# A wait in the adaLN weight ring and the order of VectorE's work around the first softmax are changed in a two-block transformer kernel

## The reference, cut to what matters

```
# first block, mixer
proj = rmsnorm(x) @ w_in                      # gq gk gr gv | mq mk | gg (gate) | mv
o_gla  = rmsnorm(gla_chunked(...)) * silu(gg) # 4 heads of 128, gated linear attention
o_moba = softmax attention over mq, mk, mv    # 8 heads of 64, causal
x = x + (concat([o_gla, o_moba]) * mix_scale) @ w_out
x = x + peer_ffn(...)
# second block, conditioning (adaLN)
mod   = silu(c) @ ada_w[l] + ada_b[l]         # ada_w[l]: 1024 x 6144, two layers
mod_c = silu(c_ctx) @ ada_w[l] + ada_b[l]
```

## Time and profile before

| what | value |
|---|---|
| median of three runs | 1842.73 us (1839.59, 1842.73, 1842.90) |
| the profiled execution | 1842.73 us, span 1840.8 us |
| TensorE matmul busy | 94% of the span |
| VectorE, ScalarE busy | 66%, 52% |
| transfers | 316 MB, mean 172 GB/s |
| mean granted TensorE clock | 0.979 of full |

### The profile page before, as it was taken

How to read it: one execution, slowest core, us unless ns; L and a number is a source line. 1 busy time by engine, 2 the same in 40 slices (tenths; PEclk the granted TensorE clock), 3 DMA queues, 4 the chain that set the end, 5 groups by cost and what they waited for, 6 DMA issues and landing times.

```text
span 1840.8 us, 37954 instructions
## 1 busy us (share of the span) xinstructions
PE 1739.4 (94%) x13770; PEld 1632.6 (89%) x13770; DVE 1211.6 (66%) x2411; ACT 949.5 (52%) x1824; POOL 77.2 (4%) x74
## 2 busy tenths in 40 slices
PE   7898999999999888999999999988999999889997
PEld 6765999999999755899999999976899999889997
DVE  5446558888854599755555566457676666767666
ACT  5444555555554588555555554337554445445442
POOL 0000000000000166100000000000000000000000
PEclk9989999999999899999999999999999999999999
DMA  6535445556556578555565555410355564546553
GB/s 235 199 138 194 149 149 177 178 182 182 177 178 185 202 283 289 172 183 182 186 203 182 182 182 155 152 44 1 115 181 182 183 207 144 155 138 183 182 182 103
DMA packets 86936, 316.38 MB, mean 172 GB/s; under 512 B 9664, under 2 KB 9808, under 8 KB 86352
## 3 DMA queue, kind: packets, MB, share of 16 engines
q1 hardware_dynamic: 85248, 309.30, 52.4%
q10 hardware_dynamic: 1328, 4.01, 0.6%
q0 software_dynamic: 288, 2.10, 0.3%
HBM read 314.32 MB, written 1.05 MB: 171 GB/s over the span
## 4 chain that ended last, share of the span: by engine, by line
PE 88%; DVE 6%; ACT 2%; issue 2%; DMA 2%; ACTq 0%; POOLq 0%; DVEq 0%
PE bank L494 30%; PE acc L494 21%; PE bank L495 15%; PE acc L495 11%; PE bank L852 4%; PE acc L571 3%; PE bank L592 1%; ACT arena L1099 1%; DMA route<-in_ada_w 1%; DVE w_lo L1584 1%; DVE small L2073 1%; ACT w_hi L1099 1%; PE bank L811 0%; ACT L1099 0%; DVE arena L2094 0%
## 5 line engine op out<-in xcount | busy, mean ns | idle before, releaser
L1584 DVE TENSOR_TENSOR w_lo<-raw,w_hi 128x512 fp32r<-128x512 f32 x982 | 652.2, 688 | 462.2 <-ACT w_hi L1099 459.5
L1099 ACT ACTIVATE w_hi<-raw 128x512 fp32r<-128x512 f32 x982 | 591.8, 626 | 429.7 <-PE acc L494 267.1
L494 PE MATMUL bank<-x_hi,w_hi 128*128 128x256 f32 x2224 | 637.1, 286 | 24.0 <-DVE w_lo L1584 17.1
L494 PE MATMUL bank<-x_lo,w_hi 128*128 128x256 f32 x2224 | 633.3, 285 | 0.0
L495 PE MATMUL bank<-x_hi,w_lo 128*128 128x256 f32 x2224 | 633.1, 285 | 0.0
L494 PEld LDWEIGHTS bank<-x_hi,w_hi 128*128 128x128 f32 x2224 | 430.1, 193 | 30.9 <-issue 17.1
L494 PEld LDWEIGHTS bank<-x_lo,w_hi 128*128 128x128 f32 x2224 | 430.4, 194 | 0.2 <-issue 0.2
L495 PEld LDWEIGHTS bank<-x_hi,w_lo 128*128 128x128 f32 x2224 | 430.4, 194 | 0.0
L494 PE MATMUL acc<-x_hi,w_hi 128*128 128x256 f32 x1024 | 290.6, 284 | 1.4 <-issue 1.4
L494 PE MATMUL acc<-x_lo,w_hi 128*128 128x256 f32 x1024 | 290.5, 284 | 0.0
L495 PE MATMUL acc<-x_hi,w_lo 128*128 128x256 f32 x1024 | 290.4, 284 | 0.0
(11 more groups left out here) (258 smaller groups left out, 1566.1 us busy)
## 6 DMA issues: line engine op xcount, KB each, us to landing
raw<-in_peer_u SPq DMA_DIRECT2D x128, 512.0 KB, 3.5
raw<-in_peer_v SPq DMA_DIRECT2D x128, 512.0 KB, 3.5
raw<-in_mlp_w SPq DMA_DIRECT2D x128, 512.0 KB, 3.6
ada_x<-in_ada_w SPq DMA_DIRECT2D x64, 512.0 KB, 4.2
route<-in_ada_w SPq DMA_DIRECT2D x32, 512.0 KB, 5.3
raw<-in_w_in SPq DMA_DIRECT2D x25, 512.0 KB, 4.5
raw<-in_conv_w_in SPq DMA_DIRECT2D x24, 512.0 KB, 4.1
raw<-in_attn_w_in SPq DMA_DIRECT2D x18, 512.0 KB, 3.5
```

The source lines that it names most:

```text
L494: return (mm(dst, a[0], b[0], start=start, stop=False, **kw), mm(dst, a[0], b[1], start=False, stop=False, **kw), mm(dst, a[1], b[0], star ...
L1099: return nc.scalar.activation(dst, src, f, **kw)
L1584: v.tensor_tensor(w_lo[:, unit(n, half)], raw[:, a:a + HALF], w_hi[:, unit(n, half)].bitcast(F32), ALU.subtract).then_inc(s["lo_done"], 1)
```

## The change

In `load_ada`, the transfer of the fourth slab of a row no longer waits for the first slab of the next row to start. It waits for the end of the row before it (`ada_row_full`), which is when the slab in its place has been read. The other slabs wait as they did. An unused argument is dropped.

On VectorE, the division of the first pair (`moba_scaled(0)`) is put ahead of the first four products of the grouped part, and the low part of tile w_out 1 is made after `moba_scaled(1)` and not between the shifts of pairs 0 and 1.

```diff
-            def load_ada(n, i=0, slot_free=False):
+            def load_ada(n, slot_free=False):
                 if n >= ADA_RING and not slot_free:
-
-                    sp.wait_ge(s["ada_started"], i * ADA_RING + (n + 2 - ADA_RING))
+                    if n % ADA_BATCH == ADA_BATCH - 1:
+                        sp.wait_ge(s["ada_row_full"], n // ADA_BATCH)
+                    else:
+                        sp.wait_ge(s["ada_started"], n + 2 - ADA_RING)
                 slot = ada_slot(n)[0]
-                sp.dma_start(ada_slots[slot], ins["ada_w"][i * ADA_RING + n]).then_inc(ada_full[slot], 16)
+                sp.dma_start(ada_slots[slot], ins["ada_w"][n]).then_inc(ada_full[slot], 16)
...
             moba_shifted(0)
-            lo(TILE["w_out"][0] + 1)
             moba_shifted(1)
+            moba_scaled(0)
             for hd in range(GLA_H):
                 a = slice((hd % 2) * 512 + (hd // 2) * T, (hd % 2) * 512 + (hd // 2) * T + T)
                 wait_full(dve, "gbc", hd)
                 v.tensor_tensor(mixed[:, hd * T:(hd + 1) * T], o_gla[:, a], B("gbc", hd)[:, 0:T], ALU.mult)\
                     .then_inc(free("gbc", hd), 1)
-            moba_scaled(0)
             for hd in range(GLA_H):
...
             moba_shifted(2)
             moba_scaled(1)
+            lo(TILE["w_out"][0] + 1)
             for c in range(4):
                 mixed_low(c)
```

## The result

The changed kernel took 1823.81 us in the median of five runs (1821.71 to 1824.35), beside 1839.59 us for the kernel before in five runs of its own (1834.9 to 1842.9). The ratio is 0.991, with a 95% interval of 0.9891 to 0.993. It is faster by 15.8 us.

A forecast was written before the change was run, and what follows sets the result against it. The prediction took TensorE, 94% busy, as the bound, with five late-slab waits and a low clock to win back. Its terms 5.34 + 3.83 + 5.2 = 14.4 us, from 1842.7, gave 1828.3 us, range 1824 to 1834.

The forecast's parts named there:

- What bounds it: Whole kernel: TensorE is 94% busy; five waits for late slabs, 19.2 us together, and a low clock behind the first.
- Row 1 and gg: First term, at slab 7: gg starts 3.86 us earlier and runs 1.48 shorter at full clock, 5.34 together.
- Row 2: Second term, at slab 11: mv starts 3.83 us earlier, with the low clock left as it is; bounds 2.3 and 8.1.
- VectorE's order: Within the third term, around the first shifts: 1.20, 0.35 and 1.63 go, so transposes 1 are released 3.2 us earlier.
- The last row: Third term, slabs 20 to 23: the stall moves to slab 21, third slab in place after 6.1; 5.2 us saved.
- rival C: Linear attention or row 2 keeps 2.4 GHz: up to 8.1 us in the second term, 1824.0 us; chance 0.06.
- clock term of 1.48: In gg behind row 1: 1.48 us taken as saved because no idle time comes ahead of gg to lower the clock.
- A: The waits go but TensorE's low clock moves elsewhere: 11.4 us gained, 1831.3 us; chance 0.15.
- B: VectorE's order wins nothing, as moba_scaled(0) waits for ScalarE or TensorE is slow; third term 2.4, 1831.1 us; chance 0.12.
- D: Slower: the clock stays at 1.2 GHz through mv and w_out, 1846.8 us at 37 us more; chance 0.03.
- E: No change: the row's end does not free the queue and something later eats the rest, 1842.7 us; chance 0.03.

The follow-up runs named there:

- busy7: The kernel before, with three matmuls of 512 columns that nothing reads put into the pause for slab 7; 1837.25 us, ratio 0.9992.
- order_only: The changed kernel's order on VectorE alone, with all slabs waiting as in the kernel before; 1835.19 us, ratio 0.9976 to the kernel before.
- before_again: The kernel before, unchanged, profiled once more in one run; its stage from the first mbc factor to w_out took 32.77 us.
- slab7_only: The kernel before with the new wait for slab 7 alone, VectorE's order as before; 1831.01 us, ratio 0.9947.
- ring_only: The changed kernel with VectorE's order put back as before, so only the new wait for the fourth slab; 1825.42 us, ratio 0.9913 to the kernel before.
- go_dense: The changed kernel with one unread matmul of 512 columns behind each half of the linear attention's products; 1824.74 us.

## Why the prediction was right or wrong

**What bounds it.** Right. The five late slabs were the waits to take away, and the low clock was the second cost.

**Row 1 and gg.** Right: 3.87 + 1.49 = 5.36, forecast 5.34. busy7 shows that the second part belongs to the pause.

**Row 2.** Right for the stall: 3.82, forecast 3.83. The clock, left as it was in the sum, fell later in the first profile, so that the linear attention's products took 1.14 less (8.07 and not 9.21), and not in the second (9.59).

**VectorE's order.** Right in mechanism and size. From the first shift (124.90) to the end of the division that releases transposes 1 (136.91) VectorE has no idle time; this takes 12.0 us where it took 15.4 (135.86 to 151.25), 3.4 less, forecast 3.2. The three pieces of 3.2 us are the low parts, a wait of 0.35 and one of 1.63. Taken alone with the stalls left in (order_only) they bring 2.4 to 2.7, and on top of the new wait 31.66 - 28.91 = 2.8. Of this the moved low part is 1.3 (forecast 1.20) and the moved division 1.4, where the two waits had been put at 1.98 together. What transposes 0 wait for is now `gbc`'s bank: they start at 131.09, and the division ended at 129.59 + 1.02 = 130.61, as the sum had it.

**The last row.** Right in mechanism: the stall moved to slab 21, where TensorE idled 1.75 (forecast some 2.5), and the third slab was in use after 6.27, forecast 6.1. The fixed cost that the prediction quoted beside it from the Trainium skill ("DMA: Bandwidth & Descriptors", anatomy of one DMA) is given there for transfers issued by GpSimd; these are issued by SyncE. The stage shrank by 5.63 between the first two profiles (34.54 to 28.91), forecast 5.2. Against the second profile of the kernel before it is 32.77 - 28.88 = 3.9. That is within the prediction's bounds of 2.4 to 6.1, so the 5.63 was in part luck: the first profile of the kernel before took 22.15 us from transposes 0 to w_out, 2 more than any other profile with the old order (19.7 to 20.3), by longer waits and low clock in about equal parts.

**The step that failed** is the base, in the sentence "I sum against the profiled execution, whose own time, 1842.73 us [...] is also the median of the runs shown". Those were three runs. The median of 53 is 1839.5, 3.2 lower, and only 12 of the 53 took 1842.7 or more. In both profiled executions of this kernel the rest of the program, where nothing is changed, took 3 to 5 us more than in eight of the other eleven profiles, and the profiled one had a mean clock as low as the slowest runs (0.979). A sum that is right to 1.4 us, subtracted from that base, lands at 1828.3; subtracted from 1839.5 it lands at 1825.1, inside the range. The forecast lies 4.5 above the measured 1823.8: 3.1 of that is the base and 1.4 the gain. The range had bounds for each term of the sum and none for the number it is taken from; its lower end was also that of rival C alone (18.7 gained), although the terms' upper bounds add up to 19.6, which is 1823.1. That the time fell just outside and not just inside is chance at 0.2 us; that it was this near the edge is the base.

**The size.** Forecast 14.4, measured 15.8 (from 12.9 to 20.1 by the interval). The stages ahead of w_out account for 16.1 between the first two profiles and for 14.4 between the second two, taken from row 0 on. What is above the forecast is in all likelihood the clock, not a wait: at the same mean clock the kernels are 11.6 apart (see before_again), where the forecast had 12.9 without its clock term of 1.48, and the other 4 us come with the higher mean clock of the changed kernel's runs. No experiment set the clock over the whole program, so this is read from the runs and not shown by one. Where each microsecond lies is open: slab7_only gained 4 us more than its two stages show, in stages whose code is the same.

**The rivals.** A (the low clock only moves) fell: gg kept full clock in every kernel without the stall. B (the middle does not move) fell: `moba_scaled(0)` did not wait for ScalarE. C in part: the linear attention's products were faster in one of two profiles of the changed kernel, but row 2 ran at the low clock in both (3.57). D and E fell: the time is shorter, and the changed kernel's mean clock is higher.

## What to carry to other kernels

When a ring of buffers is released by "the next use has started", look at where the next use starts: if it lies in another stage, release by the end of the last use instead. Here slabs 7, 11, 15 and 19, each of which had stood in the chain for 3.4 to 4.2 us, are no longer waited for. What that brings has to be read in each stage: 3.8 to 3.9 us in rows 1 and 2, with 1.5 of clock behind the first, but only 1.1 to 2.9 in the stage of rows 3 to 5 (ring_only against the two profiles of the kernel before), where VectorE's work ended last.

Before subtracting a sum from a profiled execution, ask for more runs of it, compare their mean granted clocks, and put the spread of the kernel before into the range. Here it was 12.6 us over 53 runs, almost as much as the gain, and the slow runs were those with the low clock.

A gain by medians of one part alone can be larger than its own stages show (slab 7: 9.5 against 5.4), and a stage that is 1.7 us shorter can fail to show at the end. At this size the stage's trace decides what a mechanism does, and only many runs decide what it is worth.

## What the runs showed of the hardware that was not expected

TensorE's clock fell to 1.2 GHz in the linear attention's products in all thirteen profiles, with the engine busy throughout and ahead of any stall: in the changed kernel 1.00, 0.52 and 0.50 in three windows of 2 us from 100 to 106, with 2.00 us busy in each. The two matmuls of 512 columns of go_dense came at the fall and behind it, and the clock stayed low. What in these products lets it fall was not found.

Where the clock falls differs between executions of the same kernel: in the two profiles of the kernel before the same mv projection took 13.29 and 14.82 us. "TensorE: Matmul & The Clock Gate" of the Trainium skill (its list of why this matters for kernels) names pauses between bursts as the cause of such drops. The trace and busy7 agree for the pause of 2.8 us in row 1 (gg 13.11 with it, 11.60 with the pause filled); the linear attention's products had no pause, so there the measurement goes beyond it.
